# The first attention pair of a two-stack transformer kernel: token-major projections on the raw residual, heads attended between slabs, bias spread by DMA

## What is computed

```
hn   = rms_norm(x, norm_mix_g[0])                  # 256 x 1024
proj = hn @ ab_w_in[0]                             # 1024 x 2304: qa ka va qb kb vb
qa, ka = rms_norm per head (width 64), times gain, then rotary terms
o_a  = softmax(qa ka^T / 8) va                     # 8 query heads, 2 key/value heads
o_b  = dilated attention of qb, kb, vb             # 8 heads, three branches, relative bias
h    = x + concat(o_a, o_b) @ ab_w_out[0]
```

## Time and profile before

| what | us |
|---|---|
| three runs | 1753.34, 1756.7, 1758.8 |
| median | 1756.7 |
| the profiled execution, own time | 1758.75 |
| its span in the trace | 1757.0 |
| granted PE clock, mean of the span | 0.984 |
| start, before the first projection | 0 to 20.5 |
| nine projection slabs | 20.5 to 84.0 |
| reversal of the bias | 84.0 to 91.7 |
| sixteen heads | 91.7 to 147.2 |
| two output slabs | 147.2 to 158.4 |
| `last_slabs` up to the MLP's first matmul | 158.4 to 170.4 |

### The profile page before, as it was taken

How to read it: one execution, slowest core, us unless ns; L and a number is a source line. 1 busy time by engine, 2 the same in 40 slices (tenths; PEclk the granted TensorE clock), 3 DMA queues, 4 the chain that set the end, 5 groups by cost and what they waited for, 6 DMA issues and landing times.

```text
span 1757.0 us, 24634 instructions
## 1 busy us (share of the span) xinstructions
PE 1692.7 (96%) x9735; PEld 1451.9 (83%) x9738; DVE 1078.2 (61%) x1226; ACT 846.0 (48%) x1033; POOL 25.4 (1%) x47
## 2 busy tenths in 40 slices
PE   7989999979999999999999999999999999999998
PEld 6947888775788878888997888888888999888887
DVE  4565666666566667666776766676666444556665
ACT  4244444456444455445576544464445444345443
POOL 1000000010000000000000000000000000000000
PEclk8989999999999999999999999999999999999999
DMA  9402555430355545555434554545545544235550
GB/s 374 149 0 84 216 191 191 167 129 28 120 201 190 190 172 192 193 192 189 168 109 168 188 192 183 193 178 197 192 184 180 179 181 167 87 129 193 189 192 24
DMA packets 41721, 291.90 MB, mean 166 GB/s; under 512 B 4720, under 2 KB 4864, under 8 KB 7472
## 3 DMA queue, kind: packets, MB, share of 16 engines
q1 hardware_dynamic: 38880, 281.04, 43.8%
q0 software_dynamic: 2224, 8.55, 1.3%
q10 hardware_dynamic: 544, 1.26, 0.2%
HBM read 289.76 MB, written 1.06 MB: 166 GB/s over the span
## 4 chain that ended last, share of the span: by engine, by line
PE 88%; DVE 6%; ACT 4%; issue 1%; DMA 1%; SPq 0%; ACTq 0%; DVEq 0%
PE ups L250 24%; PE accs L229 11%; PE ups L248 11%; PE accs L231 10%; PE accs L230 10%; PE ups L229 3%; PE ups L231 3%; PE ups L230 3%; DVE wlo L223 2%; PE accs L816 2%; PE ups L253 2%; ACT whi L219 1%; PE ups L795 1%; PE ups L389 1%; PE ups L1881 1%
## 5 line engine op out<-in xcount | busy, mean ns | idle before, releaser
L223 DVE TENSOR_TENSOR wlo<-raw,whi 128x2048 fp32r<-128x2048 f32 x266 | 610.5, 2297 | 225.4 <-ACT whi L219 225.3
L250 PE MATMUL ups<-xhl,whi 128*128 128x512 f32 x1824 | 634.0, 396 | 0.0
L219 ACT CAST whi<-raw 128x2048 fp32r<-128x2048 f32 x266 | 506.8, 1908 | 144.0 <-PE accs L231 76.3
L248 PE MATMUL ups<-xhl,wlo 128*128 128x256 f32 x1596 | 445.0, 279 | 0.0
L250 PEld LDWEIGHTS ups<-xhl,whi 128*128 128x128 f32 x1824 | 331.0, 188 | 64.1
L248 PEld LDWEIGHTS ups<-xhl,wlo 128*128 128x128 f32 x1596 | 300.9, 189 | 10.1
L229 PE MATMUL accs<-whi,hidh 128*128 128x512 f32 x632 | 247.5, 392 | 5.2 <-DVE hidl L770 5.2
L231 PE MATMUL accs<-whi,hidl 128*128 128x512 f32 x632 | 246.1, 389 | 0.0
L230 PE MATMUL accs<-wlo,hidh 128*128 128x512 f32 x632 | 246.0, 389 | 0.0
L229 PEld LDWEIGHTS accs<-whi,hidh 128*128 128x128 f32 x632 | 118.7, 188 | 29.4 <-issue 7.9
L231 PEld LDWEIGHTS accs<-whi,hidl 128*128 128x128 f32 x632 | 118.6, 188 | 25.1
(11 more groups left out here) (261 smaller groups left out, 2210.2 us busy)
## 6 DMA issues: line engine op xcount, KB each, us to landing
raw<-weights SPq DMA_DIRECT2D x266, 1024.0 KB, 4.8
gain<-gains POOLq DMA_DIRECT2D x10, 512.0 KB, 4.2
h<-x_in SPq DMA_DIRECT2D x2, 512.0 KB, 5.7
tabs<-consts POOLq DMA_DIRECT2D x1, 1024.0 KB, 7.2
out<-h SPq DMA_DIRECT2D x2, 512.0 KB, 2.6
tabs<-consts ACTq DMA_DIRECT2D x1, 768.0 KB, 13.2
hid<-rel_scratch POOLq DMA_DIRECT2D x1, 768.0 KB, 7.2
hidh<-rel_scratch POOLq DMA_DIRECT2D x1, 768.0 KB, 8.5
```

The source lines that it names most:

```text
L219: nc.scalar.copy(whi[:, m % SPLIT, :], raw[:, m % RAW, :]).then_inc(hi_ready, 1)
L223: nc.vector.tensor_tensor(wlo[:, m % SPLIT, :], raw[:, m % RAW, :], whi[:, m % SPLIT, :].bitcast(F32), ALU.subtract).then_inc(lo_ready, 1)
L248: nc.tensor.matmul(bank[:, 0:T], W(wlo, n, k, j * P, (j + 1) * P), xh[:, k, :], start=False, stop=False)
L250: mm = nc.tensor.matmul(bank, W(whi, n, k, j * P, (j + 1) * P), xhl[:, :, k, :], start=k == 0, stop=k == KC - 1)
```

## The change

Norm 0 becomes a raw norm: DVE multiplies x by the gain as soon as both are there; the root comes later. Slab 0 is loaded, rounded and subtracted in two halves. The first slabs are k and q (with v beside k), all token-major, so that squares, sums and rotary terms run along the free dimension on ACT and DVE; POOL multiplies the rotary tables by the gains. Normed heads are transposed on PE (`turn_kind`). The bias table is stored once per partition (2 MB instead of 16 KB) and read back already in order, so the reversal goes. Two heads at a time are attended between half slabs of the projection and of the first two output slabs. Constants that only later stages need are loaded later. Values of B heads and the unnormed q, k are scaled by the row's root when they leave PSUM. The maximum of a B head is taken in the instruction that adds the bias.

```diff
-PLAIN_NORMS = (0, 2, 4, 9)
+PLAIN_NORMS = (2, 4, 9)
@@ loads
-            for n in range(RAW):
+            sp.dma_start(raw[:, 0, 0:SLAB // 2], weights[0][:, 0:SLAB // 2]).then_inc(S("first_half"), 16)
+            sp.dma_start(raw[:, 0, SLAB // 2:SLAB], weights[0][:, SLAB // 2:SLAB]).then_inc(raw_loaded[0], 16)
+            for n in range(1, RAW):
@@ POOL
+            pool.dma_start(rope_rows[:, :], rope_gain.broadcast_to([P, 4 * HD])).then_inc(S("rope_rows"), 16)
...
+            for k in range(4):
+                nc.gpsimd.tensor_tensor(
...
             pool.wait_ge(S("rel_sum"), 1)
-            pool.dma_start(scratch[:, :], tab_sb[:, :]).then_inc(S("rel_stored"), 16)
+            spread_to = bass.AP(scratch.tensor, 0, [[REL, B_HEADS], [B_HEADS * REL, P], [1, REL]])
+            pool.dma_start(spread_to, tab_sb.unsqueeze(1).broadcast_to([B_HEADS, P, REL])).then_inc(S("rel_stored"), 16)
             pool.wait_ge(S("rel_stored"), 16)
-            for r in range(2):
...
+            diagonals = bass.AP(scratch.tensor, P - 1, [[B_HEADS * REL - 1, P], [REL, B_HEADS], [1, WIN]])
+            pool.dma_start(toep, diagonals).then_inc(S("rel_read"), 16)
@@ raw_scalar (ACT), norm 0
+            elif q == 0:
+                first_high(act)
             take_high(act, q, (0, 1, 2))
-            split_high(act, n + 1)
+            if q > 0:
+                split_high(act, n + 1)
             take_high(act, q, (3,))
+            if q == 0:
+                split_high(act, n + 1)
+                square_piece(act, s, 0)
+                square_piece(act, s, 1)
@@ raw_vector (DVE), norm 0
+            elif q == 0:
+                gain_piece(dve, q, s, 1)
+                gain_piece(dve, q, s, 2)
+                first_low(dve, 0)
+                take_low(dve, q, (0, 1))
+                first_low(dve, 1)
+                take_low(dve, q, (2,))
@@ first_tokens (PE): slab 0; part(t, first k, low) is 8 matmuls (high) or 4 (low)
+            part(0, 0, False); part(0, 0, True); part(0, 4, False); part(0, 4, True)
+            if n == 0: turn_part(pe, q, 2)
+            part(1, 0, False); turn_part(pe, q, 3); part(1, 0, True); part(1, 4, False); part(1, 4, True)
@@ ab_tensor (PE)
+            first_tokens(pe, n_ab, 0, ab_bank(0)).then_inc(slab_used, 1)
+            pe.wait_ge(lo_ready, n_ab + 2)
+            project_tokens(n_ab + 1, ab_bank(1)).then_inc(slab_used, 1)
+            table_tensor(pe)
...
+            turn_kind(0)
+            pe.wait_ge(lo_ready, n_ab + 3)
+            project_tokens(n_ab + 2, ab_bank(2)).then_inc(slab_used, 1)
+            turn_kind(1)
+            piece(3, 0)
+            scores(0)
+            piece(3, 1)
+            turn_kind(2)
+            pe.wait_ge(S("row_root"), 1)
+            turn(0)
+            for c in range(1, 6):
+                scores(c)
+                values(2 * c - 2)
+                turn(2 * c - 1)
+                piece(3 + c, 0)
+                values(2 * c - 1)
+                piece(3 + c, 1)
+                turn(2 * c)
+            scores(6); values(10); turn(11)
+            out_piece(0, blocks=(0,)); values(11); out_piece(0, blocks=(1,)); turn(12)
+            scores(7); values(12); turn(13)
+            out_piece(1, blocks=(0,)); values(13); turn(14)
+            out_piece(1, blocks=(1,), halves=(0,)); values(14); turn(15)
+            out_piece(1, blocks=(1,), halves=(1,)); values(15)
+            last_slabs(pe, n_abo + 2, ab_features(2), ab_features(3), 1,
...
@@ ab_scalar (ACT)
+            high(2); raw_root_scalar(act, 0); square(0); high(3); v_copy(0, va, P); root(0); square(1)
+            take(0); high(4); root(1); square(2); take(1); root(2); bring_table(ACT.Exp)
+            high(5); exps(0); exps(1); take(2); turned_copy(0)
+            for c in range(1, 8):
+                turned_copy(2 * c - 1); exps(2 * c); exps(2 * c + 1)
+                o_high(c - 1); high(5 + c); turned_copy(2 * c)
@@ ab_vector (DVE)
+            low(2); raw_root(dve, 0); eps_ab; sums(0); roped(0); low(3); table_vector(dve)
+            sums(1); roped(1); row_scale copy; low(4); sums(2); roped(2)
+            front(0); front(1); low(5); back(0); back(1)
+            for c in range(1, 8):
+                front(2 * c); front(2 * c + 1); plain(i); back(2 * c)
+                o_low(c - 1); back(2 * c + 1); low(5 + c)
```

More of the change, by code:

```diff
@@ L122, in after, with program @@
     return static if i is None else i * step + static
-def program(nc, weights, x, gains, columns, consts, rel_bias, lam, scratch, out):
+def program(nc, weights, x, gains, columns, consts, rel_bias, lam, rope_gain, scratch, out):
     with ExitStack() as ctx:
@@ L180, in program @@
         slab_used = sem("slab_used")
-        x_loaded = sem("x_loaded")
+        x_loaded = [sem(f"x_loaded{t}") for t in range(TB)]
         gain_loaded = sem("gain_loaded")
@@ L328, in first_slabs, with first_tokens, part @@
             project_features(n + 1, up[1]).then_inc(slab_used, 1)
+        def first_tokens(pe, n, q, bank):
+            def part(t, first, low):
+                for k in range(first, first + 4):
+                    dst = bank[:, t * T:(t + 1) * T]
+                    if low:
+                        mm = nc.tensor.matmul(dst, xl[:, k, t * P:(t + 1) * P], W(whi, n, k, 0, T), start=False,
+                                              stop=k == KC - 1)
+                    else:
+                        nc.tensor.matmul(dst, xh[:, k, t * P:(t + 1) * P], W(whi, n, k, 0, T), start=k == 0,
+                                         stop=False)
+                        nc.tensor.matmul(dst, xh[:, k, t * P:(t + 1) * P], W(wlo, n, k, 0, T), start=False,
+                                         stop=False)
+                return mm if low else None
+            if n == 0:
+                pe.wait_ge(S("first_half"), 18)
+            else:
+                pe.wait_ge(lo_ready, n + 1)
+            pe.wait_ge(xh_ready, 4 * q + 1)
+            part(0, 0, False)
+            pe.wait_ge(xl_ready, 4 * q + 1)
+            part(0, 0, True)
+            if n == 0:
+                pe.wait_ge(lo_ready, 1)
+            pe.wait_ge(xh_ready, 4 * q + 2)
+            part(0, 4, False)
+            pe.wait_ge(xl_ready, 4 * q + 2)
+            part(0, 4, True)
+            if n == 0:
+                turn_part(pe, q, 2)
+            pe.wait_ge(xh_ready, 4 * q + 3)
+            part(1, 0, False)
+            turn_part(pe, q, 3)
+            pe.wait_ge(xl_ready, 4 * q + 3)
+            part(1, 0, True)
+            pe.wait_ge(xh_ready, 4 * q + 4)
+            part(1, 4, False)
+            pe.wait_ge(xl_ready, 4 * q + 4)
+            return part(1, 4, True)
         def first_wide(pe, n, q):
@@ L834, in exps @@
                 act.wait_ge(S(nm + "_neg_max"), base + u + 1)
-                if not a["bias"] and u >= slots:
+                if u >= slots:
                     act.wait_ge(S(nm + "_turned"), base + u - slots + 1)
@@ L2198, in constants @@
     p = np.arange(P)
[L2199 to L2201 removed]
+    turn = np.arange(HD)
+    signed = np.where(turn < HD // 2, -1.0, 1.0)
+    for k, table in enumerate([np.cos(ang)[:, turn % 32], np.sin(ang)[:, turn % 32] * signed]):
+        c[:, C_TAB + k * P:C_TAB + (k + 1) * P] = table.reshape(TB, P, HD).transpose(1, 0, 2).reshape(P, TB * HD)
+    for k, table in enumerate([np.cos(angc)[:, p % 16], np.sin(angc)[:, p % 16]]):
+        c[:, C_TAB + (2 + k) * T:C_TAB + (3 + k) * T] = table.T
     for b in range(TB):
@@ L2245, in pack @@
     part = list(in_slabs(np.concatenate([wq, w[:, 512:]], axis=1)))
-    slabs += [part[k] for k in (0, 3, 1, 4, 2, 5, 6, 7, 8)]
+    slabs += [part[k] for k in (2, 0, 1, 3, 5, 7, 4, 6, 8)]
     w = i["ab_w_out"][0]
```

585 lines of the change are left out of this document (374 added, 211 removed).

## The result

The changed kernel took **1735.3 us** (median of 4 runs, 1733.6 to 1736.2) against 1757.7 for the one before in the same comparison: a ratio of 0.987, 95% interval [0.986, 0.988], 22.4 us less. The forecast was 1734. A second comparison gave 1736.0 (1734.3 to 1737.5).

What follows compares the result with a forecast made beforehand. PE, busy 96% of the span, bounds the kernel. Slab 1 to `last_slabs`: work 96.7, waits 8.0, handovers 1.5, clock 3.4, total 109.6 against 131.2; 21.6 less plus 1.0 at the start, 22.6: 1734 us, range 1722 to 1746.

Steps and rivals of the forecast that it cites:

- rival (c): Bias store on half of the 16 DMA engines takes 45 us, bias lands at 102: 10 us more, 1744; chance 0.08.
- the 768 KB row: Profiled DMA of 768 KB in 8.5 us, used as rate for the bias: store 22 us, reading back 17.
- rival (d): Slower than before: eight partitions each read 128 times, bias store 59 us or more, landing after 115; chance 0.04.
- the waits at k and q: PE waits for DVE's rotary chains before the transposes of k, 2.3 us, and of q, 1.3 us.
- the turn: One loop turn on PE: a pair's scores 1.13, two values, two transposes, two half slabs of 3.07; 10.45 us, no waits.
- the handovers: Handovers between engines from slab 1 to `last_slabs`, 15 of about 0.1 us: 1.5 us added.
- The start: Up to slab 1: first projection matmul at 13.25 us, PE waits 2.8, slab 1 at 26.2; 1.0 us gained.
- The clock: Granted clock lost after the waits of 2.8 and 3.5 us: 1.7 us each, 3.4 us added.
- Rival (b): Clock stays low through the sparse start and the loop's scores and transposes: 10 us more, 1744; chance 0.09.
- Rival (a): The pair's scores don't overlap because a semaphore or the banks order them: 8 x 1.0 us more, 1742; chance 0.08.
- Rival (e): Gain in the middle given back, since weights arrive late after a faster stage; chance 0.02.
- The edits at nothing: Later table loads, halved load of slab 0, gain of norm 1 and renumbered indices were priced at no time.

Runs made afterwards that it cites:

- not_between: dram_rows with all projection slabs first, then the heads in pairs with nothing between them, then the output slabs: 1743.2 us.
- dram_rows: The changed kernel with the 16 KB bias table stored once and spread from memory to memory as 128 whole rows: 1727.6 us, ratio 0.983.
- early_dram: dram_rows with slab 1 split on ACT and DVE before the last token tiles of slab 0: 1725.8 us.
- before_no_reversal: The kernel before the change with only the reversal of the bias taken out: 1749.4 us against 1756.5, ratio 0.996.

## Why the prediction was right, and where it was not

**The time was right (1734 against 1735.3), and so was most of the mechanism.** PE's time decides. The reversal was worth about what its gap showed (7.7 read, 7.2 measured alone, 4.2 to 9.5 by the interval); the slabs between the heads removed the waits, 15.5 us by `not_between`; taken one after the other, the medians go 1756.5 (before), 1749.4 (no reversal), 1743.2 (pairs, norms and rotations off PE, the new start), 1727.6 (slabs between), and back to 1735.3 by the late bias (these come from several comparisons, in which the kernel before had 1756.0 to 1757.7); `last_slabs` was foretold at 135.8 and came at 134.05.

**But two of its steps were off by some 7 us each and nearly cancelled; that the time came within 1.4 us is luck.**

*The bias* (rival (c), chance 0.08). At the rate of the 768 KB row the prediction put the store at 22 us and the bias in time. It took 46.6, close to the 45 that the rival named for half of the engines. That agreement is half chance: the busy share was that of half the engines, but the row's rate was far from what a well-formed copy reaches (9.7 us for 2 MB), and the source cost as much again. The row had been a read along diagonals, not the nearest kind of transfer to a store that repeats its source; the step that failed is taking one row as the rate for both. Rival (c) was priced at 10 us; it cost 7.7 to 8.3. Its bias would have landed at 102 and landed at 95.5, since the reading back took 10.7 us and not 17. What rival (d) feared, a source that is slow because it is read again and again, was there too, as the factor of 2.4, but at 46.6 us and not the 59 that it needed. With the bias in time the change gives 1727.6, 28 us less than before instead of the 22.6 foretold: the rest of the forecast was too slow by 6.4 us.

*Where the forecast was too slow.* With the bias in time `last_slabs` comes at 128.6, 7.2 us ahead of the 135.8 foretold; three terms add up to that, the other differences, each under 1 us, cancel. First, the waits at k and q (2.3 and 1.3) were zero in the changed kernel's profile and in that of `dram_rows`. In the former DVE was done with k at 34.7 us, not 35.55, since ACT's DMA issues ran beside its rounding of slab 1 (issues at 22.74 and 23.12, rounding at 23.20) and its three squares took 2.3 us, not 2.8. The larger part is that PE itself came late, at 36.19 instead of 33.25: slab 1 had started at 27.48 and run partly at the lower clock. The prediction added the clock's loss to waits that it had worked out without it, and so counted that time twice; where PE came earlier, in `early_dram`, waits of 0.59 and 0.81 were back. Second, the turn was 10.03, not 10.45, five times: scores 1.06, values 1.01 and 1.00, and the two half slabs with their transposes 6.96 (3.46 and 3.50 from start to start). Half a slab of 2.88 and transposes of 0.59, twice, make 6.94, so the changes of the matmuls' shape cost next to nothing in this turn. The prediction had weighed 0.19 a half slab for it by the later attention's row, next to what the Trainium skill, "TensorEngine Tiling (Array Packing)", Key Properties, says of a drain at a change of mode; the trace shows that price to be small here. The shorter turns are worth 2.1 us. Third, the handovers, set at 1.5 on top, are in these durations already. With the 3.6 of the waits: 7.2.

*The start.* Slab 1 was foretold at 26.2 and came at 27.48 (25.8 to 27.5 in the profiles of kernels alike up to there). The first projection matmul came at 14.11, not 13.25: the prediction let ACT copy the transposed x at once and forgot its rounding of the second half of slab 0 in front (12.44 to 13.48 us). The clock was taken to rise at about 19; matmuls follow every 0.21 us up to 18.5 and every 0.12 from 21.3 on. The wait ahead of slab 1 was 2.4 (2.8 foretold), that ahead of the first head 3.24 (3.5), values(14) 0.8 (0.9).

*The clock*, 3.4 us for two waits: slab 1 took 7.2 us instead of 5.76, 1.4 (5.9 in the second profile, where the clock did not fall); scores and values behind the first head's wait 2.04 and 1.81 instead of 1.13 and 1.08, 1.6. Together 3.1, and 1.5 more behind the wait for the bias. Rival (b), a clock that stays low, did not come: 53.65 to 90 us had 0.95.

*Rival (a)*, no overlap of the scores, was rightly thought unlikely, for a wrong reason: not the alternating order but two heads side by side make the overlap. Its price (8 us) was about right: seven pairs apart cost 7.3 in the turns, 10.5 in all. Rival (e), late weights, did not come: PE waited for none.

*The edits at nothing*: POOL's rotary tables took 2.4 us at 12.3, long before DVE's chain wanted them (33.0); the weights took 18.7 us in the median beside the store and kept nobody waiting; the MLP began right behind the 12.45 us of `last_slabs`.

**Still open**: why the medians give the bias 1 to 4 us more than the stage between the landmarks does (the time at the lower clock behind `last_slabs` is where it can lie, what sets it is not known), what makes 8 partitions a slow source, and how the start and the token-major norms share the 8.1 us by which `not_between` reaches its first scores earlier. The two weren't tried apart.

## What to carry to other kernels

Put other work of the bottleneck engine between the steps of a chain that waits for its neighbours; what it saves is the waits and the clock that is lost behind them, and waits of 3 us cost more than their length here. But ask of each transfer that the faster stage depends on from how many partitions it reads and what its outermost dimension is, and price it from a transfer of the same kind, or from both ends. Gains ahead of a transfer that is late anyway can be swallowed: the edit that gave 3.2 us with the bias in time gave 0.9 to 1.5 with it late. Mend the transfer first, then the order of the work. And do not add a loss to waits that were worked out without it: time that the busy engine loses comes out of its waits.

## What the runs showed of the hardware that was not expected

Repeating 16 KB from 8 partitions into 2 MB took 46.6, 46.7, 46.2 and 46.4 us in four profiles of three kernels; from memory, 19.5 with the same outer dimension and 9.7 as 128 rows of 16 KB. And the granted clock fell to its lower level behind waits of 3.2 to 6.0 us ahead of the heads' transposes in every profile that had one, and stayed at its upper level behind 1.4 us in all four that had that instead. Between them it went either way: behind the wait of 2.4 us ahead of slab 1 it fell in five of eight profiles, and behind one of 2.03 us ahead of a head's transposes in the kernel before, but not in `before_no_reversal`.
